# Three edits in the feed-forward parts of a transformer block: where the first chunks' halves are summed, how far ahead the weights are split, and how the tokens' parts lie

## The reference, cut to what matters

```python
y = x32 * lax.rsqrt(jnp.mean(x32 * x32, axis=-1, keepdims=True) + NORM_EPS)   # _rmsnorm, then * gain
g, u = jnp.split(h @ w_gate_up, 2, axis=-1)                                   # _swiglu, D_FF = 2816
return (jax.nn.silu(g) * u) @ w_down
```

## Time and profile before

| | us |
|---|---|
| median of three runs | 1728.63 (1727.94 to 1729.47) |
| profiled execution | 1727.93 |
| its span, first to last instruction | 1726.1 |
| TensorE busy | 1570.5 (91%) |
| DVE busy | 938.5 (54%) |
| ACT busy | 675.4 (39%) |
| POOL busy | 288.9 (17%) |
| mean granted TensorE clock | 0.981 |

### The profile page before, as it was taken

The page is one execution under the profiler, slowest core; times in us unless marked ns, Lnnn a source line. Parts: engine busy times, 40 slices in busy tenths (PEclk is TensorE's granted clock), DMA queues, the critical chain, the costliest instruction groups (busy, mean ns, idle before and its releaser), DMA issues.

```text
span 1726.1 us, 32447 instructions
## 1 busy us (share of the span) xinstructions
PE 1570.5 (91%) x13304; PEld 1327.7 (77%) x13305; DVE 938.5 (54%) x1551; ACT 675.4 (39%) x1002; POOL 288.9 (17%) x215
## 2 busy tenths in 40 slices
PE   8999987776676667999999999999999999999998
PEld 8889974443333334899999888999899998989997
DVE  5765741111111112876678467667766677476665
ACT  6454421100000001554455554444544455554443
POOL 1020030000000000111115411122211116311111
PEclk9999999999989999999999999999999999999999
DMA  8544599999999999355567445555355566345551
GB/s 334 182 147 147 224 408 429 428 428 428 429 429 428 428 428 427 127 190 191 187 224 251 172 147 183 184 183 218 148 184 183 183 254 236 143 161 183 184 183 62
DMA packets 42554, 435.24 MB, mean 252 GB/s; under 512 B 5067, under 2 KB 5195, under 8 KB 7764
## 3 DMA queue, kind: packets, MB, share of 16 engines
q1 hardware_dynamic: 41716, 429.56, 63.8%
q0 software_dynamic: 736, 4.22, 0.7%
HBM read 430.59 MB, written 3.16 MB: 251 GB/s over the span
## 4 chain that ended last, share of the span: by engine, by line
PE 71%; DMA 14%; DVE 6%; SPq 4%; issue 2%; ACT 1%; POOL 1%; ACTq 0%; DVEq 0%
PE bank L1116 17%; PE bank L661 11%; DMA ring<-moe_w_dram 11%; PE bank L663 11%; PE bank L662 11%; PE bank L1118 9%; SPq L440 4%; PE bank L1046 2%; DMA area<-moe_w_dram 2%; PE bank L1070 1%; POOL area L573 1%; PE bank L997 1%; PE bank L1224 1%; DVE lo_last L1910 1%; DVE lo_first L1910 1%
## 5 line engine op out<-in xcount | busy, mean ns | idle before, releaser
L1116 PE MATMUL bank<-h_split,w_hi 128*128 128x512 f32 x1408 | 499.6, 395 | 9.5 <-DVE area L2355 3.5
L1116 PEld LDWEIGHTS bank<-h_split,w_hi 128*128 128x128 f32 x1408 | 264.6, 188 | 69.8 <-issue 6.3
L1612 ACT CAST w_hi<-ring 128x2048 fp32r<-128x2048 f32 x120 | 227.5, 1896 | 58.7 <-PE bank L663 55.5
L573 POOL TENSOR_TENSOR area<-area,stat 128x256 f32<-128x256 f32 x88 | 146.5, 1665 | 589.4 <-DVE area L2357 589.4
L1118 PE MATMUL bank<-h_split,lo_last 128*128 128x256 f32 x864 | 244.1, 283 | 0.0
L662 PE MATMUL bank<-hid_lo,w_hi 128*128 128x256 f32 x704 | 199.9, 284 | 0.0
L661 PE MATMUL bank<-hid_hi,w_hi 128*128 128x256 f32 x704 | 197.9, 281 | 0.0
L1910 DVE TENSOR_TENSOR lo_last<-ring,w_hi 128x2048 fp32r<-128x2048 f32 (+1 forms) x74 | 165.0, 2230 | 35.2 <-ACT w_hi L1612 35.2
L1118 PEld LDWEIGHTS bank<-h_split,lo_last 128*128 128x128 f32 x864 | 162.4, 188 | 0.1
L661 PE MATMUL bank<-h_split,w_hi 128*128 128x256 f32 x556 | 161.7, 291 | 0.9 <-DVE h_split L1902 0.9
L1618 ACT CAST w_hi<-ring 128x1024 fp32r<-128x1024 f32 x88 | 92.4, 1050 | 163.7 <-PE bank L663 163.7
(11 more groups left out here) (440 smaller groups left out, 3154.3 us busy)
## 6 DMA issues: line engine op xcount, KB each, us to landing
ring<-layer_w_dram SPq DMA_DIRECT2D x120, 1536.0 KB, 6.6
ring<-moe_w_dram SPq DMA_DIRECT2D x88, 1536.0 KB, 36.8
area<-moe_w_dram SPq DMA_DIRECT2D x40, 1536.0 KB, 36.9
ring<-first_w_dram SPq DMA_DIRECT2D x21, 1536.0 KB, 6.6
bias_copies_dram<-bias_rows_dram POOLq DMA_DIRECT2D x1, 2048.0 KB, 11.8
h_t<-area SPq DMA_DIRECT2D x32, 64.0 KB, 4.2
ring<-first_w_dram SPq DMA_DIRECT2D x3, 512.0 KB, 6.6
x_t<-x_dram SPq DMA_DIRECT2D x1, 1024.0 KB, 5.0
```

The lines of the kernel that those rows point to most:

```text
L573: pool.tensor_tensor(up, up, stat[:, 3, :], ALU.mult).then_inc(S("up_scaled"), 1)
L1116: pe.matmul(halves(first_bank + side), hi_of(q)[:, cols], h_split[:, :, k, :], start=k == 0, stop=False, skip_group_check=True)
L1612: act.copy(hi_of(q)[:, part_a], ring[:, PLACES[q % len(PLACES)], part_a]).then_inc(S("hi_a_ready"), 1)
```

## The change: what it does, and the diff

It has three edits, and no arithmetic changes.

1. In ACT's queue the copies of the second halves of chunks 0 and 1 move: chunk 0's ahead of the square root for the norm (in the very first part behind it, ahead of the silu table), chunk 1's behind chunk 0's silu. In DVE's queue the sum of chunk 0's halves moves ahead of the norm's factor (of its reciprocal, in the very first part), and that of chunk 1 into chunk 0, behind lo_b.
2. hi_a and lo_a in the loop now treat slot c+3, not c+2, and begin in chunk 0; none is left for chunk 21.
3. h_split becomes block by block: for each k the high block and at once the low one, and the 512-wide matmul reads 512 columns in one run. wide_hi and wide_lo follow (six blocks in the ring slot, two in h_split).

```diff
+WIDE_HERE = 6
...
-             "h_split": (2, KB, T), "hid_hi": (3, T), "hid_lo": (3, T)}, 0)
-        h_hi, h_lo = h_split[:, 0], h_split[:, 1]
+             "h_split": (KB, 2, T), "hid_hi": (3, T), "hid_lo": (3, T)}, 0)
+        h_hi, h_lo = h_split[:, :, 0, :], h_split[:, :, 1, :]
...
-                        pe.matmul(halves(first_bank + side), hi_of(q)[:, cols], h_split[:, :, k, :],
+                        pe.matmul(ps[first_bank + side], hi_of(q)[:, cols], h_split[:, k].rearrange("p a t -> p (a t)"),
...
+                if at:
+                    copy_halves(0)
+                    norm_root(value, ACT.Silu)
+                else:
...
+                    copy_halves(0)
+                    act.activation(lbs[:, 1:2], lbs[:, 4:5], ACT.Silu)
+                for c in range(CHUNKS):
+                    n = CHUNKS * (2 * layer + f) + c
+                    if c > 1:
+                        copy_halves(c)
                     if c < CHUNKS - 1:
                         hi_b(at + c + 1)
                     act.wait_ge(S("gate_scaled"), n + 1)
                     sg = gate_pair[:, n % 2, 0, :]
                     act.activation(sg, sg, ACT.Silu).then_inc(S("silu_done"), 1)
-                    if c:
-                        hi_a(at + c + 2)
+                    if c == 0:
+                        copy_halves(1)
+                    if c < CHUNKS - 1:
+                        hi_a(at + c + 3)
...
                 if at:
                     squares_summed(value)
                     lo_a(at + 2)
+                    sum_halves(0)
                     own(rms_factor(value))
                 else:
                     first_factor()
+                    sum_halves(0)
+                    own(dve.reciprocal(stat[:, 3, :], stat[:, 0, :]))
                 for c in range(CHUNKS):
...
+                    if c > 1:
+                        sum_halves(c)
...
                     lo_b(at + c)
+                    if c == 0:
+                        sum_halves(1)
...
                         .then_inc(S("hid_made"), 1)
-                    if c:
-                        lo_a(at + c + 2)
+                    if c < CHUNKS - 1:
+                        lo_a(at + c + 3)
```

More of the change, by code:

```diff
@@ L299, in wide_hi @@
         def wide_hi(k):
-            return lo_last[:, 0, (8 + k) * T:(9 + k) * T] if k < 4 else h_hi[:, k - 4, :]
+            return lo_last[:, 0, 2 * k * T:(2 * k + 1) * T] if k < WIDE_HERE else h_hi[:, k - WIDE_HERE, :]
         def wide_lo(k):
-            return lo_last[:, 0, k * T:(k + 1) * T]
+            return lo_last[:, 0, (2 * k + 1) * T:(2 * k + 2) * T] if k < WIDE_HERE else h_lo[:, k - WIDE_HERE, :]
         def ab_hi(k):
@@ L1652, in swiglu, with copy_halves @@
                 hi_b(at)
[L1653 to L1660, removed]
+                def copy_halves(c):
                     n, first_bank = CHUNKS * (2 * layer + f) + c, GATE_BANKS[c % 2]
@@ L1666, in swiglu @@
                         .then_inc(S("halves_copied"), 1)
+                if at:
+                    copy_halves(0)
+                    norm_root(value, ACT.Silu)
+                else:
+                    act.wait_ge(S("var_ready"), 4)
+                    act.activation(stat[:, 0, :], stat[:, 1, :], ACT.Sqrt, bias=bias_mean, scale=1.0 / D)\
+                        .then_inc(S("std_ready"), 1)
+                    copy_halves(0)
[4 more added lines that the diff above has]
+                        copy_halves(c)
                     if c < CHUNKS - 1:
@@ L1972, in first_factor @@
                 dve.wait_ge(S("std_ready"), 4)
-                own(dve.reciprocal(stat[:, 3, :], stat[:, 0, :]))
             def residual_scaled(p):
@@ L2344, in swiglu, with sum_halves @@
                 value = 3 * layer + 1 + 2 * f
+                def sum_halves(c):
+                    n, first_bank = CHUNKS * (2 * layer + f) + c, GATE_BANKS[c % 2]
+                    dve.wait_ge(S("halves_copied"), n + 1)
+                    both = gate_pair[:, n % 2]
+                    tt(both, bank[:, first_bank:first_bank + 2, 0:T], both, ALU.add).then_inc(S("halves_summed"), 1)
                 if at:
@@ L2350, in swiglu @@
                     first_factor()
+                    sum_halves(0)
+                    own(dve.reciprocal(stat[:, 3, :], stat[:, 0, :]))
                 for c in range(CHUNKS):
[L2352 to L2355, removed]
+                    n = CHUNKS * (2 * layer + f) + c
+                    if c > 1:
+                        sum_halves(c)
+                    sg, hid = gate_pair[:, n % 2, 0, :], gate_pair[:, n % 2, 1, :]
                     dve.wait_ge(S("halves_summed"), n + 1)
```

## The result

| | before | changed |
|---|---|---|
| median of 8 runs | 1728.39 us | 1734.10 us |
| lowest to highest | 1727.74 to 1732.44 | 1729.60 to 1735.40 |
| ratio, 95% interval | | 1.0026 (1.0016 to 1.0035) |
| profiled execution, span | 1727.93, 1726.1 us | 1734.59, 1732.8 us |
| TensorE busy | 1570.5 us | 1580.4 us |

The change made the kernel slower by 0.26%, 4.5 us, where 0.26% faster was forecast. The medians lie 5.7 us apart, the means 4.5; the text goes by the ratio. 1734.1 lies 0.1 us outside the range.

A forecast was written before the change was run, and what follows sets the result against it. Bound: the order of TensorE's own work in the feed-forward parts and mixers. Starts -9.6, holes +10.4, clock +1.7 and one-run reads -7.0 gave -4.5 us, from 1728.6 to 1724.1 us; range 1711 to 1734.

The forecast's parts named there:

- edit 3's 7 us of gain: 512-wide matmuls reading one run instead of two: each about 5 ns less over 1408 matmuls, 7 us gained.
- Stalls at the starts: Chunks 2 and 3 of the four feed-forward parts: eight TensorE stalls go, with their restarts, 9.6 us gained.
- Steady part: Middle chunks of a part: ACT waits about 1 us for DMA in every chunk, hidden, cost 0.
- The hole at the end: Before chunk 21's down product in three of four parts: TensorE waits nearly 4 us, 10.4 us lost in all.
- The granted clock: After the three new holes: one fall to half speed for 3.4 us taken, between none and three, 1.7 us lost.
- the gap that the prediction held against it: Expert stage: one of two 2.19 us TensorE gaps was followed by matmuls at the full 2.4 GHz.
- a sign of being wrong: 512-wide and 256-wide matmul pair: forecast 346 ns; keeping 351 ns or falling under 340 would refute it.
- Rival 2: 512-wide matmul: one run reaches the pace of line 646's matmuls, 216 ns, 21 us gained, total 1710 us; chance 0.10.
- Rival 1: 512-wide matmul: one run is no faster than two, so no gain there, total 1731 us; chance 0.28.
- rival 4: Three part ends: holes bring the clock down, 1.7 us each; without the layout gain, three falls give 1734.5 us; chance 0.11.

The follow-up runs named there:

- e4: Kernel before plus edit 1 and, of edit 2, only slot 3 split early in chunk 0, old layout: 0.9933 of before, 1717.61 us.
- e7: Changed kernel with slots 22 and 23 split in chunks 20 and 21 as before, none in chunk 19: 0.9936 of before, 1718.25 us.
- e8: Changed kernel with 8 calls of unread matmuls filling each of the three holes before the last down product: 1.0007 of before.
- e5: Kernel before with only slot 23's split moved from chunk 21 to chunk 20: 1.0084 of before, 14.5 us slower.
- e1: Kernel before with edit 3 alone, high and low tokens side by side: 1.0004 of before.
- e9: e4's order in the new layout, without the 256-wide product of the weights' low part: 233 ns from one 512-wide matmul's start to the next.
- e10: e4's order in the old layout, without the 256-wide product of the weights' low part: 233 ns from one 512-wide matmul's start to the next.
- e6: Changed kernel with 16 calls of unread matmuls put into each of the three holes before the last down product: 1.0073 of before.

## Why the prediction was wrong, point by point

The step that made the sign wrong is edit 3's 7 us of gain, which measured nothing; the falls of the clock were priced at under half, and the holes a little low.

- **Stalls at the starts: right.** 9.6 us were forecast and the parts are 10.0 us shorter. All eight stalls went, in the changed kernel and in e4.
- **Steady part: the cost of 0 is right, the length of the wait is not.** ACT does wait for DMA in nearly each chunk. The forecast put the wait at "about 1 us", counted from gate_up's end, and the trace counts 2.6 us a time (193.2 us in 74), as ACT asks earlier. e7 shows that the waits are hidden.
- **The hole at the end: right in place, cause and number.** Three of them, none in the last part, hidden rows ready at 889.12 where 889.45 was worked out. The size was a little low: 3.4 us of shift a hole were forecast, while the way from part 2 to part 3 and that from part 3 to part 4 are 3.9 and 3.7 us longer in e8 than in e7, and neither met a fall there. The first way is 4.0 longer, less the 1.5 of e8's fall in the mixer: 11.5 us in all for the forecast 10.4.
- **The granted clock: the rule was there, the price was halved.** The step "between no fall and three I take one, 1.7 us" failed. In the changed kernel, edit 2 alone (e3) and the hole alone (e5), nine holes of 3.4 to 3.9 us came with nine falls, two of them of 6.8 us. The three of the changed kernel are worth 3.3 us by e8's time and 4.0 by its trace. The forecast's own price, half the length of a fall, would make their 3.4, 6.8 and 3.4 us worth 6.8: that price was not reached. In the second stretch above TensorE was busy for 5.86 of 6.80 us; why the rest did not cost its half is not shown. The page TensorE: Matmul & The Clock Gate of the Trainium skill (HAM oscillation) has such waits bring the clock down; here the trace agrees, nine times in nine. The waits that the page shows are longer than 2.19 us, so the gap that the prediction held against it does not contradict it.
- **Edit 3: this step made the sign wrong.** The 7 us came from carrying the 13.3 ns overhead of a 256-wide matmul to a 512-wide one. That was a comparison of two different widths, and nothing in it said that the second run was the cause of the rest. e1 measured 0.7 us of loss with 0 inside, e9 and e10 the same 233 ns, and the pair kept its 351 ns, which the prediction had named as a sign of being wrong. Rival 2's pace of 216 ns is out too: it was read from rows of line 646 that are halves of a plain f32 matmul (last section), and the page TensorE: Matmul & The Clock Gate of the Trainium skill (Back-to-back issue gap) gives the formula for the isolated gap and says that in a stream of weight loads and matmuls both set the spacing. The trace has such a stream at 233 ns. Rival 1 priced "no gain", and rival 4 (no gain from edit 3, three falls: 1734.5) is what happened, at a chance of 0.11. That 1734.5 comes so near the measured 1734.1 is in part luck: its falls are priced 1 us too high and its holes 1 us too low.

With each term as the traces have it (starts, holes, falls, edit 3), -10.0 + 11.5 + 4.0 + 0 = +5.5 us. Measured was +4.5, with 2.8 to 6.0 in the interval.

## What to carry to other kernels

A prefetch that goes one step deeper changes what a strict queue waits for: ask for every instruction behind it how long it can be late, and ask it again at the end of the loop, where the work that covered it is missing. Here one deeper step was wanted only at the start: edit 1 with slot 3 split early, and the rest left two ahead, gave 0.9933 where the whole change gave 1.0026. A term that rests on another form's overhead is a guess about its cause; it should not decide the sign of a forecast.

## What the runs showed of the hardware that had not been expected

- The granted clock in the expert stage stayed up after one 2.19 us gap and fell after the other, but came down with every one of nine gaps of 3.4 to 3.9 us that follow dense matmuls. With fillers in the gap it fell after none of six (e6, e8). What length between decides was not tried.
- In the mixers the clock falls in some executions and not in others, without any gap of TensorE: layer 0's at 982.4 above, layer 1's in the earlier trace rows, neither in e7. Such a fall is worth 1.5 us (3.4 us long; e1 against before and e7) to 3.1 (6.8 long; before against e7), as much as half of what was to be measured here, and what brings it on is open.
- A plain f32 matmul of 256 columns stands in the trace as two rows of 216 ns each: 8 calls made 16 rows, 16 made 32, and (7.07 - 0.38) / 31 = 0.216 us. The rows of line 646 are therefore halves of a matmul (its two calls and then six show as 4 and 12 rows), which makes them a poor yardstick for the fp32r one.
